# The output projection of a hybrid decoder layer as seven block products for each pair of token tiles

## The reference

```python
x = x + mixed @ w_out              # mixed: 512 x 1024, w_out: 1024 x 1024
u = rmsnorm(x, norm_ffn)
p_group = softmax(u @ wg + bg)     # 4 groups, one is taken
e_logits = u @ we + be             # 8 experts in the group, two are taken
y = sum over chosen experts of w * (silu(u @ w_gate) * (u @ w_up)) @ w_down
out = rmsnorm(x + y, norm_final)
```

## Time and profile before

| what | value |
|---|---|
| median of three runs (lowest, highest) | 1066.2 us (1065.35, 1066.5) |
| profiled execution, its own time | 1067.21 us |
| its span, first to last instruction | 1065.4 us |
| busy share of PE, PE weight load, DVE, ACT | 96%, 68%, 52%, 29% |
| mean granted TensorE clock | 0.984 |
| bytes moved | 174.76 MB, mean 164 GB/s |

### The profile page before, as it was taken

One profiled execution on the slowest core, in us unless ns is written; L12 is line 12 of the kernel. 1 busy time (PEld: TensorE's weight loads), 2 busy tenths in 40 slices (PEclk: granted clock), 3 DMA queues, 4 the chain that ended last, 5 costly groups with the idle time before them and its releaser, 6 DMA issues. The chain is left out here.

```text
span 1065.4 us, 20882 instructions
## 1 busy us (share of the span) xinstructions
PE 1022.0 (96%) x8985; PEld 725.4 (68%) x8985; DVE 551.7 (52%) x1088; ACT 310.3 (29%) x579; POOL 112.5 (11%) x109
## 2 busy tenths in 40 slices
PE   9999999999999999999999999999999999787887
PEld 8888888777877878877775676444466665545544
DVE  6577786869468388397364464423244322111124
ACT  2445354534343343353332132100110111100013
POOL 3322222000000000001001000000001222111110
PEclk9999999999999999999999999999989999988999
DMA  9232222232242142241222222075757999999976
GB/s 265 68 82 68 61 61 76 65 65 60 61 84 62 41 84 62 60 85 43 60 60 60 60 61 67 33 276 194 326 197 263 412 415 414 415 416 414 417 301 247
DMA packets 111967, 174.76 MB, mean 164 GB/s; under 512 B 9011, under 2 KB 87100, under 8 KB 103554
## 3 DMA queue, kind: packets, MB, share of 16 engines
q1 hardware_dynamic: 99010, 134.93, 36.9%
q10 hardware_dynamic: 7136, 27.33, 6.5%
q0 software_dynamic: 5728, 11.14, 4.0%
HBM read 169.16 MB, written 12.60 MB: 171 GB/s over the span
## 5 line engine op out<-in xcount | busy, mean ns | idle before, releaser
L824 PE MATMUL ps<-arena 128*128 128x256 f32 x1008 | 237.6, 385 | 0.0
L824 PEld LDWEIGHTS ps<-arena 128*128 128x128 f32 x1008 | 185.2, 190 | 27.3 <-issue 2.8
L1518 DVE TENSOR_TENSOR arena<-arena 128x256 f32<-128x256 f32 (+6 forms) x202 | 111.3, 592 | 46.4 <-ACT arena L1309 32.7
L854 PE MATMUL ps<-arena 128*128 128x264 f32 x400 | 124.0, 392 | 0.8 <-DVE gates L1650 0.8
L2421 PE MATMUL ps<-arena,gates 128*64 128x256 f32 (+1 forms) x1088 | 106.8, 355 | 15.6 <-DMA arena<-in_expert_w_up 14.9
L855 PE MATMUL ps<-arena 128*128 128x264 f32 x400 | 121.7, 386 | 0.0
L2421 PEld LDWEIGHTS ps<-arena,gates 128*64 128x64 f32 x1088 | 74.1, 145 | 54.6 <-DMA arena<-in_expert_w_up 24.3
L848 PE MATMUL ps<-yT,arena 128*128 128x512 f32 x192 | 84.8, 596 | 2.1 <-DVE gates L1650 1.4
L855 PEld LDWEIGHTS ps<-arena 128*128 128x128 f32 x400 | 76.0, 190 | 13.0
L854 PEld LDWEIGHTS ps<-arena 128*128 128x128 f32 x400 | 71.7, 190 | 13.1 <-issue 2.8
L2600 DVE COPY gates<-ps 128x1024 f32<-128x1024 f32 x15 | 18.4, 1224 | 102.2 <-PE ps L2402 102.1
(11 more groups left out here) (379 smaller groups left out, 1402.9 us busy)
## 6 DMA issues: line engine op xcount, KB each, us to landing
arena<-in_w_in SPq DMA_DIRECT2D x68, 512.0 KB, 3.9
arena<-in_expert_w_gate SPq DMA_DIRECT2D x27, 1024.0 KB
arena<-in_expert_w_up SPq DMA_DIRECT2D x27, 1024.0 KB
arena<-in_expert_w_down ACTq DMA_DIRECT2D x16, 1024.0 KB, 33.3
arena<-in_w_branch SPq DMA_DIRECT2D x12, 512.0 KB, 4.3
arena<-in_expert_w_down SPq DMA_DIRECT2D x6, 1024.0 KB, 27.8
C<-in_expert_w_gate SPq DMA_DIRECT2D x5, 1024.0 KB
gates<-in_expert_w_up SPq DMA_DIRECT2D x5, 1024.0 KB
```

The lines of the kernel that those rows point to most:

```text
L824: mm = t.matmul(dst, wt[:, k, :], rhs[:, k, :], start=(k == 0), stop=(k == KH - 1))
L854: t.matmul(dst[:, 0:HALF], wt, uT[:, k, 0:HALF], start=(k == 0), stop=(k == KD - 1))
L1518: v.tensor_tensor(out_, a_, b2, op).then_inc(*q.did(name))
```

## The change

The output projection is done as two block products, one for each pair of token tiles p (tiles 2p and 2p + 1). Inner dimension (k = 0 to 3, 4 to 7) and output columns (0 to 511, 512 to 1023) are halved, and each 2 x 2 block product takes seven products of half size in place of eight: P1 to P7, each four matmuls of 128x512. The sums that go into them are made by DVE: three of halves of `w_out` in the middle of the merge (T1, T2, T3), four of tokens for each pair behind it (S1, S2, S4, S3), and T4. The sums T1, T2 and T4 need 6144 words of each partition at the start of `arena`, which was the buffer of expert 2's weights (expert 1 and 2 change places); token sums of pair 1 stand in `yT[:, 8:12]`, which was the buffer of expert 4's down weights. So SP loads expert 2 after the last product P4.1, and expert 4's down weights after `lg`. x is loaded before the weights of expert 0. DVE adds the parts to the residual in 22 steps instead of 8; ACT copies the two P1 products out of PSUM.

```diff
-            for n in range(KD):
+            for n in range(KD // 2):
                 merged_last(n)
+            v.wait_ge(sem("out_w"), 16)
+            v.tensor_tensor(mixed_wo[:, 0], wo[:, 0:KH, 512:], wo[:, 0:KH, 0:512], ALU.subtract).then_inc(*out_mix.did("T1"))
...
+            for n in range(KD // 2, KD):
+                merged_last(n)
+            v.wait_ge(*m_dve.after(f"h{KD - 1}"))
+            for p in range(2):
+                row = [[gates[:, i * KH:(i + 1) * KH, (2 * p + j) * P:(2 * p + j + 1) * P] for i in range(2)] for j in range(2)]
+                s1, s2, s3, s4 = (mixed_rows[p][:, n] for n in range(4))
+                v.tensor_tensor(s1, row[1][0], row[1][1], ALU.add).then_inc(*out_mix.did(f"S1.{p}"))
...
+            v.tensor_tensor(mixed_wo[:, 2], wo[:, KH:, 0:512], mixed_wo[:, 1], ALU.subtract).then_inc(*out_mix.did("T4"))
...
                 sp.dma_start(wo, w_out[0].rearrange("(k p) d -> p k d", p=P)).then_inc(sem("out_w"), 16)
+                sp.wait_ge(sem("block_done"), where["m", "ab", KD - 1] + 1)
+                sp.dma_start(h, x[0].rearrange("(i p) d -> p i d", p=P)).then_inc(sem("x_again"), 16)
                 load_weights(sp, 0, 0)
...
+                    dst, lhs, rhs = {"P1": (bank(p), gates[:, 0:KH, tile[0]], wo[:, 0:KH, 0:512]),
+                                     "P2": (bank(2 + p), gates[:, KH:KD, tile[0]], wo[:, KH:, 0:512]),
+                                     "P3": (bank(6), s4, wo[:, KH:, 512:]),
+                                     "P4": (bank(4 if p else 0), gates[:, KH:KD, tile[1]], mixed_wo[:, 2]),
+                                     "P5": (bank(1 if p else 4), s1, mixed_wo[:, 0]),
+                                     "P6": (bank(5), s2, mixed_wo[:, 1]),
+                                     "P7": (bank(7), s3, wo[:, 0:KH, 512:])}[name]
...
+                for name in ("P1", "P2"):
+                    for p in range(2):
+                        out_part(name, p)
+                for name in ("P5", "P6", "P3", "P7"):
+                    out_part(name, 0)
+                turn_tokens(0, every, "T0")
+                out_part("P4", 0)
+                out_part("P5", 1)
+                turn_tokens(1, every, "T1")
+                logits(0, every, "t0")
+                out_part("P6", 1)
+                out_part("P3", 1)
+                logits(1, every, "t1")
+                out_part("P7", 1)
                 turn_tokens(2, every, "T2")
-                out_product(7, range(0, KD - 2))
+                out_part("P4", 1, range(0, 2))
+                turn_tokens(3, high_half, "T3b")
+                out_part("P4", 1, range(2, KH))
+                logits(2, every, "t2").then_inc(*pe2.did("l2"))
                 turn_tokens(3, low_half, "T3a")
...
+                v.tensor_tensor(u, bank(5), u, ALU.add).then_inc(*dve2.did(f"U{p}"))
+                v.wait_ge(*dve2.after(f"U{p}"))
+                v.tensor_tensor(both_parts, bank(1 if p else 4), u, ALU.add).then_inc(*dve2.did(f"V{p}"))
+                add(f"h{n + 1}a", n + 1, both_parts, dve2.after(f"V{p}"))
+                add(f"h{n + 3}a", n + 3, both_parts)
+                add(f"h{n + 2}a", n + 2, u)
+                add(f"h{n + 1}", n + 1, bank(6), pe2.after(f"P3.{p}"), dve2.after(f"h{n + 1}a"))
+                add(f"h{n + 3}", n + 3, bank(7), pe2.after(f"P7.{p}"), dve2.after(f"h{n + 2}a"))
+                add(f"h{n + 2}b", n + 2, bank(7))
...
-            weights = [in_one(ARENA - KD * D - WX), in_one(0), in_one(WX), in_one(ARENA - WX),
+            weights = [in_one(ARENA - KD * D - WX), in_one(WX), in_one(0), in_one(ARENA - WX),
...
-                for n in (1, 2):
-                    load_weights(sp, n, n)
+                load_weights(sp, 1, 1)
                 load_gate(sp, 4, 4)
-                load_down(sp, 4, 4)
                 load_gate(sp, 5, 5)
...
-                sp.wait_ge(*pe2.after("o7"))
+                sp.wait_ge(*pe2.after("P4.1"))
+                load_weights(sp, 2, 2)
                 load_weights(sp, 3, 3)
                 load_second(sp, 4, 4)
+                sp.wait_ge(*pe2.after("lg"))
+                load_down(sp, 4, 4)
                 sp.wait_ge(sem("rows_kept"), 16 * NT)
```

More of the change, by code:

```diff
@@ L2037, in tail @@
             c_w = [small(NT), small(NT)]
+            first_part = [gates[:, 8, :], arena[:, 2 * 3 * 2 * D:2 * 3 * 2 * D + 512]]
+            both_parts = gates[:, 17, :]
+            last_rows = mixed_rows[1][:, 0]
             def sync(sp):
@@ L2086, in turn_tokens, with logits @@
                     mm.then_inc(*pe2.did(name))
-                def logits(i, ks, copied):
+                def logits(i, ks, copied, first=0, last=KD - 1):
                     t.wait_ge(*dve2.after(copied))
                     for k in ks:
-                        mm = t.matmul(logit_bank(i), u2T[:, k, i * P:(i + 1) * P], wr[:, k, :],
-                                      start=(k == 0), stop=(k == KD - 1))
-                    return mm
-                def out_product(n, ks):
-                    i = n // 2
-                    for k in ks:
[L2099 to L2103, removed]
+                        rows = last_rows[:, k - KH] if i == NT - 1 and k >= KH else u2T[:, k, i * P:(i + 1) * P]
+                        mm = t.matmul(logit_bank(i), rows, wr[:, k, :], start=(k == first), stop=(k == last))
+                    return mm
@@ new lines, in out_part @@
+                def out_part(name, p, ks=range(KH)):
+                    tile = [slice((2 * p + j) * P, (2 * p + j + 1) * P) for j in range(2)]
+                    s1, s2, s3, s4 = (mixed_rows[p][:, n] for n in range(4))
+                    if ks[0] == 0:
+                        if name == "P5":
+                            t.wait_ge(*out_mix.after(f"S1.{p}"))
+                            if p:
+                                t.wait_ge(*act2.after("r1"))
+                        if name == "P6":
+                            t.wait_ge(*out_mix.after(f"S2.{p}"))
+                        if name == "P3":
+                            t.wait_ge(*out_mix.after(f"S4.{p}"))
+                        if name == "P7":
+                            t.wait_ge(*out_mix.after(f"S3.{p}"))
+                        if name == "P4":
+                            t.wait_ge(*out_mix.after("T4"))
+                            if p == 0:
+                                t.wait_ge(*act2.after("r0"))
+                    dst, lhs, rhs = {"P1": (bank(p), gates[:, 0:KH, tile[0]], wo[:, 0:KH, 0:512]),
[5 more added lines that the diff above has]
+                                     "P7": (bank(7), s3, wo[:, 0:KH, 512:])}[name]
+                    for k in ks:
+                        if p == 0 and name in ("P1", "P2"):
+                            t.wait_ge(*m_dve.after(f"h{k if name == 'P1' else KH + k}"))
+                        mm = t.matmul(dst, lhs[:, k, :], rhs[:, k, :], start=(k == 0), stop=(k == KH - 1))
+                    if ks[-1] == KH - 1:
+                        mm.then_inc(*pe2.did(f"{name}.{p}"))
```

90 lines of the change are left out of this document (51 added, 39 removed).

## The result

| | before | changed |
|---|---|---|
| median of 5 runs, us | 1066.2 (1065.35 to 1066.5) | 1060.81 (1060.36 to 1061.14) |
| ratio, 95% interval | | 0.995 (0.9936 to 0.9965) |
| profiled execution, span / time, us | 1065.4 / 1067.21 | 1059.3 / 1061.14 |

The gain is 5.4 us by the medians and 6.1 by the two profiled executions. The same kernel in a second comparison: 1060.13 against 1064.7 us, 0.9962 (0.9948 to 0.9975), 4.6 us. The forecast was 4.9 us off the profiled execution and a median of 1061.6 us (range 1057.2 to 1064.9).

What follows compares the result with a forecast made beforehand. The expert weight stream was taken as the bound: loads 7.9 us earlier plus 6.5 idle minus 10.2 for 4.19 MB gave 4.2 us, by bytes 6.7; 4.9 was taken, for a median of 1061.6 us, range 1057.2 to 1064.9.

Steps and rivals of the forecast that it cites:

- What bounds the kernel: Long expert stage: it ends when its stream of weights ends, at 412 GB/s, with PE waiting for weights.
- The projection: PE's output projection: 56 matmuls in place of 64 save 6.9 us, a 1.35 us hole closes; router 8.9 us earlier.
- DVE: Sums and adds in the projection: 2.3 us per 2048-element sum, hidden behind waits and products, PE not held up.
- The loads start: SP's first load behind the row write of tile 2: at 777.4 against 785.27, 7.9 us earlier.
- idle transfer time: Transfer gaps ahead of the dense weight stream, to be squeezed out: 6.5 us by DMA shares, 9.0 by bytes.
- the start of PE's experts: PE's first expert work: near 799 to 800 us, with expert 6's gate weights wanted at about 804.
- The whole PE gain: Rival at the experts' start: the extra 4 MB finds room, the end moves 8.9 us to 1057.3 us; chance 0.13.
- The row write behind the weights: Rival before the row fetch: tile 3's write lands at 800.3, experts start 2.0 us later, 1068.2 us; chance 0.07.
- The projection saves less: Rival in the projection: DVE work or half clock delays PE and loads, each us costing 1 us; chance 0.13.

Runs made afterwards that it cites:

- fill_late_before_p4: fill_to_fetch with four idle matmuls (3.4 us of PE) ahead of P4.1, so late loads and experts both come later; 1064.91 us, 1.0003 of the kernel before.
- fill_late_behind_p4: fill_to_fetch with the same four idle matmuls behind P4.1 and the logits of tile 2, so the late loads keep their time; 1060.99 us, 0.9966.
- hold_back_4mb: Changed kernel with up and down weights of experts 4 and 5 (4.2 MB) asked for only once the first two row fetches have landed; 1063.74 us, 0.9993.
- fill_to_fetch: Changed kernel with ten filler matmuls instead of five between the router's last product and the first fetched rows; 1060.63 us, 0.9965 of the kernel before.
- loads_late_alone: Kernel before with only expert 2's weights and expert 4's down weights loaded behind the last output product (4.2 MB); 1067.62 us, 1.003.
- sums_6us_more: Changed kernel with the sum T1 made four times (6.9 us more of DVE); 1062.85 us, 0.9979 of the kernel before.
- early_and_hold: Changed kernel with loads asked for once their buffers are free, but expert 5's up and down (2.1 MB) held until two row fetches landed; 1056.56 us, 0.9919.

## Why the prediction was right, and where not

**What bounds the kernel** was right. That the stream sets the end, and not PE, is shown by fill_late_before_p4 against fill_late_behind_p4, by hold_back_4mb and by fill_to_fetch. loads_late_alone does not bear on it.

**The projection** was right to within 0.7 us. Forecast: last product done at 776.7, router at 781.1; measured: logits behind it at 776.05, router at 780.97, 9.1 us earlier. Most of the 0.7 is that the projection starts 0.7 us earlier, at 721.35.

**DVE** was right. Forecast 2.3 us for a sum of 2048 elements, measured 2.29. The Trainium skill ("VectorE: DVE Perf Modes", The TRN2 errata) gives a formula for this add in fp32, (N + 151) / 0.96 ns; at 2048 it is 2291 ns, and the trace agrees. T1 to T3 end at 719.95 (forecast 720.7), h1 at 746.3 ahead of T0 at 748.81, `wn` waited for nothing. That the cover was real, and how thick, is shown by sums_6us_more.

**The loads start** at 776.81, 8.5 us earlier; forecast 777.4 and 7.9.

**The term that was mis-sized is the idle transfer time.** The prediction had 6.5 us by shares and 9.0 by bytes, and stayed "near" the shares, for a gain of 4.9. The measured 5.4 = 8.5 - 10.2 + x gives x = 7.1 us; the profiled pair's 6.1 gives 7.8, and the 4.6 of the second comparison about 6, so the size of the miss is itself uncertain by about 1 us. The account by bytes was the better one for when the transfers run out: 7.65 + 4.19 MB at 412 GB/s are 28.7 us, from 778.7 to 807.4; the forecast by shares said about 810. In the trace the share stays at 1.02 up to 806 and is 0.97 in the window behind it.

**The step that failed** is the start of PE's experts, "near 799 to 800", and with it expert 6 "wanted at about 804". The forecast moved the whole chain by 8.9 us, though it knew that the fetch would run beside weights. The fetch is at 794.36, 9.0 us earlier, but takes 7.2 us to PE in place of 4.3. Its price goes with the load beside it: 3.45 us with share 0.31 (early_and_hold), 4.3 with share 0.76 (before), 6.7 to 8.7 in the versions with weights in flight. From PE's start to the request for expert 6 it is then 5.7 us, at clock 0.50; at 1.00 it is 3.65 (fill_to_fetch, 800.00 to 803.65). So the 5 us that expert 6 was to lie in the queue were not there: it was asked for at 807.25, just as the transfers ran out. That this changed nothing (fill_to_fetch) was luck, not foresight: any later, and PE would have been the bound.

**The rivals.** *The whole PE gain* did not come, as argued, for want of room for 4 MB. A gain of that size was there to be had, 8.7 us in early_and_hold, but not by this rival's way: there expert 6 was asked for 13 us earlier than before (799.83), and that the two figures are near each other is chance. *The row write behind the weights* fell: it landed at 788.2, 7.7 us after its issue, with eight loads of 1.049 MB asked for between 776.8 and 781.6. The prediction expected a landing near 790 by the Trainium skill's rule that a DMA engine takes turns between queues by packets ("DMA: Bandwidth & Descriptors", Queues, rings and completion order); the trace agrees, as far as one landing can: last in turn, the write would have landed at about 800. *The projection saves less* did not happen: the products run from 721.35 on without a wait, at granted clock 1.00. The mechanism is real, though: with 3.4 us lost there, fill_late_before_p4 keeps nothing of the gain (1.0003).

## What to carry to other kernels

When a stage ends on a stream of weights, count the bytes that must be through before the stream's next request, and the idle transfer time ahead of it: a faster engine gains only what the late loads leave, and here loads that started 8.5 us earlier, with 4.19 MB more among them, brought 5.4 us. Then look for the small transfer on the critical chain: holding 2 MB back for two fetches gained 1.8 us by the medians (not clear of the noise) where the chain was late, and holding 4 MB back cost 3 us where the stream was. Which of the two holds is read from one row, the DMA share between the end of the preloads and the first request for a freed buffer.

## What was not expected of the hardware

A row fetch from GpSimd took 3.45 us to PE with the transfers mostly idle and 7.2 us beside a dense stream on another queue (up to 8.7 in loads_late_alone); GpSimd spends 1.09 us on issuing it in both, so the difference lies behind the issue.

The stretch of half clock in the router is not tied to the kernel. The trace of before and that of the changed kernel both have it, so it is not in the difference between them. Windows of the same filler matmuls, changed kernel and fill_to_fetch, whose edit lies behind it:

```profile
779.70:786.50 6.80, 6.80 (x14) 3.53 (x14) 5.57 (x23) 0.22 (x1) 0.00 (x0) 0.50 0.99 350
```

```profile
779.70:786.50 6.80, 6.64 (x23) 3.30 (x22) 6.11 (x23) 0.22 (x1) 0.00 (x0) 1.00 0.99 335
```

With this stretch at 0.50 (1.2 GHz) the router takes 13.4 us from its first step to the fetch (780.97 to 794.36), with it at 1.00 (2.4 GHz) 11.0 (781.26 to 792.24). In both the engine did the same work ahead of it, so what made the clock fall in one of the two stays open.
